# Moving small sums, scores and norm steps later among the weight units of a hybrid mLSTM and SSD decoder layer

## What is computed

```python
x = x + 0.5 * g1 * swiglu(u, ff1_w1, ff1_w3, ff1_w2)
mq, mk, mv, mo, mi, mf, z, xbc, dtp, ga, gb = split(u @ w_in)
qk = silu(causal_conv(concat(mq, mk)))
lf = log_sigmoid(f_pre)                    # gates, from mi, mf; dt = softplus(dtp)
b = cumsum(lf)                             # the gates' sums
mt = maximum(b + m, max_s(b_t - b_s + i))  # running maxima, the gates' rows
s = (q @ k.T) * exp(b_t - b_s + i - mt)    # the scores of a head
...
gated = ys * silu(z)
gg = gg * rsqrt(mean(gg * gg) + EPS)       # group norm, 4 groups of 512 channels
yb = (gg * s_norm_g) @ w_pb
merged = sigmoid(ga) * ya + sigmoid(gb) * yb
x = x + g2 * (merged @ w_out)
x = x + 0.5 * g3 * swiglu(u, ff2_w1, ff2_w3, ff2_w2)
```

## Time and profile before

| | |
|---|---|
| median of 3 runs | 1346.93 us (1343.83 to 1350.98) |
| the profiled execution's own time | 1344.18 us |
| its span, first to last instruction | 1342.5 us |
| TensorE (PE) busy | 1273.4 us, 95% |
| VectorE (DVE) busy | 767.6 us, 57% |
| ScalarE (ACT) busy | 618.3 us, 46% |
| GpSimd (POOL) busy | 214.7 us, 16% |
| mean granted TensorE clock | 0.984 |

### The profile page before, as it was taken

One profiled execution on the slowest core, in us unless ns is written; L12 is line 12 of the kernel. 1 busy time (PEld: TensorE's weight loads), 2 busy tenths in 40 slices (PEclk: granted clock), 3 DMA queues, 4 the chain that ended last, 5 costly groups with the idle time before them and its releaser, 6 DMA issues. The chain is left out here.

```text
span 1342.5 us, 22663 instructions
## 1 busy us (share of the span) xinstructions
PE 1273.4 (95%) x9096; PEld 1160.1 (86%) x9096; DVE 767.6 (57%) x1340; ACT 618.3 (46%) x1067; POOL 214.7 (16%) x377
## 2 busy tenths in 40 slices
PE   5899999998999999989999999999899999999997
PEld 2799999997988676768998879788899979999997
DVE  1644445336875566665389686865375565545433
ACT  3433334334667554645355664554652343333442
POOL 4100000002540321211033232311500010000010
PEclk9899999999999999999999999999999989999999
DMA  9956776785343588883674456364336464444551
GB/s 308 260 187 222 221 232 199 224 251 169 119 126 126 190 272 299 302 292 112 173 220 126 128 164 180 111 197 130 107 96 188 143 203 157 151 139 131 151 150 41
DMA packets 258862, 241.56 MB, mean 180 GB/s; under 512 B 8607, under 2 KB 242479, under 8 KB 258710
## 3 DMA queue, kind: packets, MB, share of 16 engines
q1 hardware_dynamic: 249262, 211.03, 51.7%
q0 software_dynamic: 9024, 28.91, 6.2%
q10 hardware_dynamic: 472, 0.17, 0.1%
HBM read 209.88 MB, written 30.21 MB: 179 GB/s over the span
## 5 line engine op out<-in xcount | busy, mean ns | idle before, releaser
L2108 DVE TENSOR_TENSOR w_lo<-ring,w_hi 128x1024 fp32r<-128x1024 f32 (+1 forms) x264 | 336.2, 1275 | 426.8 <-ACT w_hi L1536 426.5
L1536 ACT ACTIVATE w_hi<-ring 128x1024 fp32r<-128x1024 f32 (+1 forms) x264 | 289.5, 1097 | 542.4 <-PE bank L826 535.2
L826 PE MATMUL bank<-u_hi,w_hi 128*128 128x320 f32 x1536 | 277.8, 324 | 7.4 <-ACT u_hi L1561 5.1
L826 PEld LDWEIGHTS bank<-u_hi,w_hi 128*128 128x128 f32 x1536 | 239.6, 194 | 25.8 <-issue 19.6
L826 PE MATMUL bank<-u_lo,w_hi 128*128 128x320 f32 x1536 | 260.6, 313 | 0.0
L826 PE MATMUL bank<-u_hi,w_lo 128*128 128x320 f32 x1536 | 256.2, 309 | 0.0
L826 PEld LDWEIGHTS bank<-u_lo,w_hi 128*128 128x128 f32 x1536 | 238.2, 192 | 0.0
L826 PEld LDWEIGHTS bank<-u_hi,w_lo 128*128 128x128 f32 x1536 | 233.4, 188 | 0.0
L628 POOL TENSOR_TENSOR arena<-arena 128x320 f32<-128x320 f32 x24 | 20.9, 872 | 610.0 <-ACT arena L1548 599.6
L823 PE MATMUL aux<-ident,arena 128*128 128x128 f32 (+6 forms) x404 | 60.4, 273 | 14.4 <-ACT arena L1593 8.7
L826 PE MATMUL bank<-arena 32*128 32x128 f32 (+5 forms) x536 | 57.1, 373 | 14.1 <-DMA arena<-in_state_mlstm_C 6.8
(11 more groups left out here) (362 smaller groups left out, 1510.6 us busy)
## 6 DMA issues: line engine op xcount, KB each, us to landing
ring<-in_w_in SPq DMA_DIRECT2D x52, 1024.0 KB, 5.4
ring<-in_ff_w SPq DMA_DIRECT2D x44, 1024.0 KB, 5.5
ring<-in_ada_w SPq DMA_DIRECT2D x36, 1024.0 KB, 7.6
ring<-in_ff_w SPq DMA_DIRECT2D x32, 704.0 KB, 4.8
arena<-in_state_mlstm_C SPq DMA_DIRECT2D x32, 512.0 KB, 5.1
out_s_C<-arena POOLq DMA_DIRECT2D x32, 512.0 KB, 5.8
ring<-in_w_pa SPq DMA_DIRECT2D x8, 1024.0 KB, 8.1
arena<-in_state_ssm SPq DMA_DIRECT2D x32, 256.0 KB, 3.9
```

The lines of the kernel that those rows point to most:

```text
L826: return nc.tensor.matmul(dst, lhs, rhs, start=first, stop=last)
L1536: nc.scalar.activation(w_hi[v.split_no % 2][:, 0:v.kc, :], panel_part(v), ACT.Copy).then_inc(S["hi_done"], 1)
L2108: V.tensor_tensor(w_lo[r][:, 0:v.kc, :], panel_part(v), w_hi[r][:, 0:v.kc, :].bitcast(FP32), ALU.subtract)\
```

## The change

Nine places in the order are moved, on four lists. No operation is added or removed.

- `gate_sums` goes from behind qk unit 7 to behind unit 8, `rows_out` from behind 11 to behind 12, and ScalarE's `row_exponents` with it.
- `scores(1)` goes from behind the unit v 1 into the unit v 2, between its second and third part.
- In the tail `group_sums(0)` goes from behind unit 1 to 2, `group_sums(1)` and `(2)` from 2 to 3, `group_roots(0..2)` from 3 to 4, `group_sums(3)` from 5 to 6, and `group_roots(3)` from 8 to 10. On ScalarE and VectorE the roots go from 2 to 3 and from 6 to 8.
- VectorE's low halves go one unit later, from the unit of their high halves to the next, and with them the wait for `tail_sent`; the last two stand behind the loop.

```diff
-            def dense(u, high=u_hi, low=u_lo, late=None):
+            def dense(u, high=u_hi, low=u_lo, late=None, inner=None, behind=1):
...
                 for kc, row in enumerate(u.rows):
                     mm(bank, w_hi[r][:, kc, :], low[:, row, :], False, False)
+                if inner and behind == 2:
+                    inner()
                 pe.wait_ge(S["lo_done"], u.split_no + 1)
...
-                if u.q == 7:
+                if u.q == 8:
                     gate_sums()
-                if u.q == 11:
+                if u.q == 12:
                     rows_out()
...
-                dense(st.at[name_q])
+                dense(st.at[name_q], inner=(lambda: scores(1)) if i == 2 else None, behind=2)
...
                     keys(i)
-                    scores(i)
+                    if i != 1:
+                        scores(i)
...
-                if i == 1:
+                if i == 2:
                     group_sums(0)
-                if i == 2:
+                if i == 3:
                     group_sums(1)
                     group_sums(2)
-                if i == 3:
+                if i == 4:
                     for gr in range(3):
                         group_roots(gr)
-                if i == 5:
+                if i == 6:
                     group_sums(3)
-                if i == 8:
+                if i == 10:
                     group_roots(3)
...
-                if u.own == 11:
+                if u.own == 12:
                     row_exponents()
...
-                if i == 2:
+                if i == 3:
                     roots(0, 3)
...
-                if i == 6:
+                if i == 8:
                     roots(3, 4)
...
-                if i == 2:
+                if i == 3:
                     group_roots(0, 3)
-                if i == 6:
+                if i == 8:
                     group_roots(3, 4)
                 if i >= 4:
                     for c in range(2 * (i - 4), 2 * (i - 4) + 2):
                         group_norm(c)
-                    if i == 4:
-                        for r in range(2):
-                            dve.wait_ge(tail_sent[r], 5 * 32)
-                    for c in range(2 * (i - 4), 2 * (i - 4) + 2):
+                if i == 5:
+                    for r in range(2):
+                        dve.wait_ge(tail_sent[r], 5 * 32)
+                if i >= 5:
+                    for c in range(2 * (i - 5), 2 * (i - 5) + 2):
                         group_norm_low(c)
+            for c in (14, 15):
+                group_norm_low(c)
```

More of the change, by code:

```diff
@@ L867, in dense @@
                     mm(bank, w_hi[r][:, kc, :], high[:, row, :], row == 0, False)
+                if inner and behind == 1:
+                    inner()
                 for kc, row in enumerate(u.rows):
                     mm(bank, w_hi[r][:, kc, :], low[:, row, :], False, False)
+                if inner and behind == 2:
+                    inner()
                 pe.wait_ge(S["lo_done"], u.split_no + 1)
```

## The result

The kernel after takes 1337.72 us (median of 20 runs, 1335.74 to 1346.8) and the kernel before, beside it, 1346.78 us (20 runs, 1342.05 to 1350.98). The ratio is 0.9938, with a 95% interval of 0.9925 to 0.9950. So the change wins 9.1 us by the medians and 8.4 us by the ratio, and lies just outside the 0.5% that stood for no change. The forecast was 1333.7 us, 13.2 us less than before. The direction and the range hold, the size is 4 to 5 us too large.

What follows compares the result with a forecast made beforehand. TensorE, busy for 95% of the span, was taken as the bound, so only its idle and low-clock time could be won. Terms of 2.8 + 1.5 + 8.9 = 13.2 us gave 1333.7 us from 1346.93, range 1328 to 1341.

Steps and rivals of the forecast that it cites:

- Query and key units (2.8): Gates' sums one unit later: 1.30 us wait and 1.7 us low clock go, 0.2 lost; 2.8 us, bounds 1.5 to 3.0.
- Scores and row units (1.5): Scores of head 1 inside unit v 2: wait falls from 3.09 to 0.8 us; 1.5 us won, bounds 0 and 1.6.
- ScalarE's circle of 8.36 us: Row units: ScalarE and VectorE work takes 8.36 us per unit, so TensorE leaves at most 1.5 us earlier.
- First and fourth sums (3.2 + 6.2): Tail: later group sums no longer wait for GpSimd; idleness and low clock saved, 3.2 us at the first, 6.2 at the fourth.
- Low halves (0.5): Tail: VectorE-ScalarE circle of norms and weights, 4.0 us per unit, starts about 966, not 976; 0.5 us lost to short waits.
- the signs that I had named for being right: Among them: no waits before the moved sums, VectorE's send wait under 3 us, first `pb` unit 13 us earlier.
- the send lands 6 us late: Tail: the bound of 4.8 us on the loss at the low halves; the other bound was none.
- A: Tail paced by VectorE, ScalarE and the send: tail wins 4.3 us, total gain 8.6, time 1338.3 us; chance 0.17.
- B: Waits only move: row units give nothing, VectorE halves the first gain, A holds; 5.8 us, 1341.1 us; chance 0.09.
- C: Low clock drawn anew behind six stalls that the change leaves alone: 20.4 us lost, time 1354.1 us; chance 0.04.
- D: More than forecast: all 17.3 us come, or another stall loses its low clock; 15 to 18 us, about 1330; chance 0.12.
- The rule on table switches: Tail, root of group 3: draining adds 1.38 us per table switch, 2.66 in all; by it the gain would be 11.4 us.

Runs made afterwards that it cites:

- the kernel without the zeroing in it: Kernel after, with the send's wait behind the tail's loop and ScalarE's zeroing of value rows taken out of the row units: 1333.38 us, 0.9894 of before.
- control 2: Kernel after, unchanged, timed again in the group with the queries' and keys' edits taken back: 1336.96 us, 0.9930 of before.
- control 1: Kernel after, unchanged, timed again beside the moved zeroing and two kernels with the send's wait moved: 1335.66 us, 0.9926 of before.
- the two first parts alone: Two kernels: before with only the queries' and keys' edits (1347.29 us, 0.9999), and before with only the scores of head 1 moved (1345.42 us, 0.9984).

## Why the prediction was right, and where it was off

**Query and key units (2.8).** The wait went as described, and VectorE did not become the bound: the one wait for a low weight near there is of 0.2 us, at 372 to 374 us in five of the eight traces with the new order. Alone the edits measured 0.1 us won by the ratio (2.4 won to 2.2 lost by its interval), and taking them back cost 3.1 us. The term's weak half is the clock. Five of the profiled kernels have the sums at the old place, and TensorE waited 1.28 to 1.31 us there in each. The half clock followed in two (before, and the tail alone) and not in three (scores alone, send wait moved in before, and these edits taken back). So of 1.7 us for the clock the mean over executions is nearer to 0.7, and the term nearer to 2.0. The stretch itself says 1.8: from the gate products to the first row unit the five traces with the old place take 69.3 to 70.9 us, 70.0 in the mean, and the eight with the new one 68.0 to 68.3, 68.2 in the mean. Neither timing tells 2.0 from 2.8, or the first from 0.

**Scores and row units (1.5).** Right. The trace gives 1.5 us (from the first row unit to `denominators`), the run alone 1.3. The bound from ScalarE's circle of 8.36 us was the right one, as the kernel without the zeroing in it showed. The waits of 0.56 and 0.95 us before the scores of heads 2 and 3 came as predicted.

**First and fourth sums (3.2 + 6.2).** Right: 9.2 us ahead at the end of unit 7 for 9.4. One reading was off without harm. The prediction had the fourth sums asked for 7.8 us behind the end of unit 4, 0.7 us after their input. It left out that the three `group_roots` (2.98 us on TensorE) now stand in between too. They are asked for at 970.53 us, and GpSimd's sum was done at 967.00, 3.5 us earlier. The 3.4 us of low clock in the 6.2 are those of one execution; over the three traces with the tail of before the mean lead is 9.6 us.

**Low halves (0.5): here it failed.** The step "That is close: I take 0.5 us of short waits" was worth 4.9 us. Two things in it were wrong. I had the issue of the last send right (about 6 us earlier; 5.7 measured from the end of unit 1), but let its landing come earlier by as much. It flew 4.7 us and not 1.8, so VectorE got on only 2.8 us earlier. The circle did start at about 966 us (967.92 in the trace after, 966.3 by the clock of the trace before), since its first low weight now stands ahead of the wait. But I let it run through from there, and the wait of 3.84 us stood inside its first turn. And I checked the delayed circle only against the first `pb` units, where TensorE needs the low halves. It needs the circle three units earlier, since each unit waits for a bank that ScalarE's gate frees. Moving this one wait gives the 8.9 back in the trace, three times out of three. Two of the signs that I had named for being right failed with this step: VectorE's wait for the send was not below 3 us, and the first `pb` unit came 8.8 us earlier (4.5 and 4.3) and not 13.

The other end of that step's bounds, 4.8 for "the send lands 6 us late", has the right size by luck: the send flew 2.9 us longer, and the loss is that of the three gates and of the half clock behind the last one (0.79 over 8 us, 1.7 us), which the step did not have. An estimate from the trace after says that the slow flight is what let the gates bite: with a flight of 1.8 us everything behind VectorE's wait moves up by 2.9 us, and the three waits for gates add up to 2.75. No run shows that order with a fast send.

**The rivals.** A forecast 1338.3 us from a tail that wins 4.3 us, "if the last send lands no earlier than now". Its picture held: the wait for the send stays, and the circle starts anew behind it. Its condition did not, since VectorE went on 2.8 us earlier, so that its price came out in part by luck. What spoke against it in the text, that the send hangs on ScalarE's unit 4, was true of the issue and not of the landing; 0.17 was too little for it. B is out by the row units' 1.6 us; its halved first gain is near the mean of 1.8 us for the query and key units, but VectorE's list was not what halved it. C did not strike, and D did not come.

**The rule on table switches.** In the kernel after ScalarE's timeline has the root of group 3, with its table and the table for the gate, inside the circle:

```profile
983.48 1.28 ACT L2008 ACT_TABLE_LOAD   x1
984.78 0.27 ACT L2008 ACTIVATE sm<-aux,eps_col 128x2 f32<-128x2 f32 x1
...
987.80 1.28 ACT L1900 ACT_TABLE_LOAD   x1
989.10 0.44 ACT L1900 ACTIVATE arena<-bank 128x320 f32<-128x320 f32 x1
```

Each load takes 1.28 us, and the next function starts 0.02 us behind it. The second load is what TensorE's wait of 1.49 us ends on. The 2.66 us that the Trainium skill gives in "ScalarE: Activation LUTs", section "What ACT_TABLE_LOAD costs", are not seen here either. By an estimate from that figure, 1.38 us more for each of the two switches, the wait before unit 11 could not have shrunk to 0.28 us once the send's wait was gone.

**Not settled.** In the traces moving the send's wait wins 4.5 to 5.1 us of the tail, idleness and clock together, in each of three executions, against three of the kernel after. In the totals it wins about 1: 0.9927 and 0.9918, against 0.9938, 0.9926 and 0.9930 for the kernel after. The intervals reach 0.17 to 0.27% (2.3 to 3.6 us) to either side, that of the kernel after's 20 runs 0.13%. The clock helps a little to split this up. Span times (1 - clock) is what full speed would have saved, span times clock the rest; means over the timed runs, with twice the standard error:

| kernel | low clock us | rest us |
|---|---|---|
| before (three groups) | 23.0 (0.8), 23.4 (1.2), 24.0 (1.0) | 1322.6 (0.8), 1322.7 (1.2), 1321.8 (1.1) |
| queries' and keys' edits alone | 24.3 (1.0) | 1321.1 (1.2) |
| after, and its two controls | 18.1 (0.8), 16.7 (1.5), 18.0 (1.2) | 1319.2 (1.0), 1317.9 (1.3), 1317.5 (0.7) |
| after without queries' and keys' edits | 19.1 (1.2) | 1320.0 (1.4) |
| send wait moved, and with the low halves old | 18.3 (0.6), 17.8 (0.6) | 1317.3 (2.1), 1315.8 (1.0) |

The idleness arrives: moving the send's wait takes about 1.6 us off the rest, the queries' and keys' edits take 1.5 off alone and 2.5 beside control 2. The low clock does not go down with the send's wait (18.3 and 17.8 against 16.7 to 18.1), though the traces have one stretch of 1.7 us less in the tail. For the queries' and keys' edits the two pairs disagree: 24.3 with them against 23.0 without, but 18.0 with them against 19.1 without. So a part of the gain at the clock may come back elsewhere. Whether it does, or these are draws, 6 to 12 runs for a kernel don't tell.

## What to carry to other kernels

- A wait that is hidden behind a longer one has no price until the longer one goes. Moving the send's wait was worth nothing in the kernel before and 4.5 us of the tail in the traces of the kernel after, of which the totals show about 1. When an edit takes a stall away, follow the next wait on every engine of the circle to each thing that it frees: weights, halves and PSUM banks.
- A transfer's landing has a time of its own. If it is issued earlier, ask what else is issued then; here a small send issued just behind a large load took 4.7 us and not 1.8.
- Price a stretch at the low clock by how often it follows such a stall, not by the one trace in which it did.

## What the runs showed of the hardware

- **The half clock does not follow every short stall.** With stalls of 1.28 to 1.31 us before the gates' sums it followed in two of five profiled executions, with those of 1.53 us before the first group's sums in two of four. With those of 3.05 to 3.16 us (the scores of head 1 at the old place) it followed in four of four, and with those of 1.48 to 1.49 us, the last gate of the tail, in all six executions that have it. The last stands behind other waits for gates. In the kernel before a part of a unit took 2.33 us at the half clock (at 975.37 us) and 1.34 at the full one. The Trainium skill, "TensorE: Matmul & The Clock Gate", Part 1, says that the chip's view of activity runs freely of the kernel, so that the same kernel varies. The stalls of 1.53 us agree: they come behind the same list of work in all four traces. The loads of state, with three half-clock stretches in the kernel after and two in control 1, are weaker evidence, since the first stall differed too (2.10 and 0.91 us).
- **A small send beside a large load.** In the kernel after, its two controls, the tail alone and the one with the queries' and keys' edits taken back the last send of 48 KB was issued 0.3 us behind a load of 1 MB into `ring`, and VectorE, waiting for it, went on 4.6 to 5.4 us after the issue. In the kernel before, the two first parts alone and the one with low halves and send wait at their old place, where no load is issued close ahead, it went on after 1.9 us. In the four with the send's wait behind the loop nothing waits for it, and it landed 3.7 to 5.5 us after its issue, with the load 0.1 to 0.3 us ahead. I did not move the load by itself, so that it is the cause is argued from these thirteen traces.
